# Memory's norm moved from the last gate block into the gated and differential products, and the head turns put behind the gated blocks

## What is computed

```python
z = h @ w_in[l]
u_s, q, k, v, g = jnp.split(z, [COL_SSM, COL_Q, COL_K, COL_V], axis=-1)
ys = s5_branch(u_s, ...)
ys = jax.nn.gelu(ys)
ys = ys * jax.nn.sigmoid(ys @ w_glu[l] + b_glu[l])            # gated product
branch_a = ys @ w_ssm_proj[l]
ya = diff_attention(q, k, v, ...)                             # 8 heads, each normed and scaled
branch_b = ya @ w_da_proj[l]                                  # differential product
gates = jax.nn.sigmoid((g + b_gate[l]).astype(F32))
g_a, g_b = jnp.split(gates, 2, axis=-1)
merged = (g_a * branch_a + g_b * branch_b)
x = x + rms_norm(merged @ w_mix_out[l], norm_mix_post[l])
...
mem_n = rms_norm(mem, norm_mem[l])                            # memory's norm: 256 rows of 1024
kv = mem_n @ w_xkv
```

## Time and profile before

| | us |
|---|---|
| median of 3 runs (2285.89 to 2286.31) | 2285.9 |
| the profiled execution's own time | 2281.14 |
| its span | 2279.5 |
| PE busy in the span (95%) | 2162.6 |
| DVE, ACT, POOL busy | 1123.0, 1005.2, 792.6 |
| chain that ended last: PE's share | 77% |

### The profile page before, as it was taken

How to read it: one execution, slowest core, us unless ns; L and a number is a source line. 1 busy time by engine, 2 the same in 40 slices (tenths; PEclk the granted TensorE clock), 3 DMA queues, 4 the chain that set the end, 5 groups by cost and what they waited for, 6 DMA issues and landing times.

```text
span 2279.5 us, 31042 instructions
## 1 busy us (share of the span) xinstructions
PE 2162.6 (95%) x11196; PEld 1775.5 (78%) x11196; DVE 1123.0 (49%) x2003; ACT 1005.2 (44%) x1950; POOL 792.6 (35%) x347
## 2 busy tenths in 40 slices
PE   5999999799989989999998999999999999999997
PEld 4788888678887878888886877878777777777776
DVE  5789999452542356452436523222286623222374
ACT  5767777652343442222223333434633433444631
POOL 2511111334464134444442423232343432232342
PEclk9999999899999999999998999999999999999998
DMA  4211111233233122232322222222223222222221
GB/s 145 84 61 65 64 60 60 74 120 102 93 126 96 38 83 74 94 100 93 102 92 88 93 65 75 68 72 71 87 84 125 83 84 64 67 69 71 76 94 63
DMA packets 51732, 189.32 MB, mean 83 GB/s; under 512 B 6564, under 2 KB 7204, under 8 KB 51108
## 3 DMA queue, kind: packets, MB, share of 16 engines
q1 hardware_dynamic: 48096, 175.13, 23.8%
q10 hardware_dynamic: 2452, 6.88, 0.8%
q0 software_dynamic: 1072, 5.77, 0.7%
HBM read 185.66 MB, written 2.10 MB: 82 GB/s over the span
## 4 chain that ended last, share of the span: by engine, by line
PE 77%; DVE 10%; ACT 5%; issue 3%; DVEq 3%; POOL 2%; DMA 0%; ACTq 0%; POOLq 0%
PE bank L350 21%; PE bank L352 20%; PE bank L351 20%; PE bank L933 2%; PE bank L976 2%; POOL weight_lo L382 1%; PE bank L959 1%; ACT weight_hi L376 1%; DVE wide_region L2225 1%; ACT wide_region L1059 1%; DVE wide_region L2228 1%; PE bank L425 1%; DVE h_lo L399 1%; PE bank L604 1%; PE bank L637 1%
## 5 line engine op out<-in xcount | busy, mean ns | idle before, releaser
L382 POOL TENSOR_TENSOR weight_lo<-weight_slots,weight_hi 128x1024 fp32r<-128x1024 f32 x277 | 674.6, 2436 | 1045.5 <-ACT weight_hi L376 1039.9
L376 ACT ACTIVATE weight_hi<-weight_slots 128x1024 fp32r<-128x1024 f32 x272 | 288.0, 1059 | 806.0 <-PE bank L352 720.3
L350 PE MATMUL bank<-h_hi,weight_hi 128*128 128x512 f32 x1144 | 464.5, 406 | 4.3 <-issue 3.0
L351 PE MATMUL bank<-h_lo,weight_hi 128*128 128x512 f32 x1144 | 449.6, 393 | 0.0
L352 PE MATMUL bank<-h_hi,weight_lo 128*128 128x512 f32 x1136 | 446.5, 393 | 0.0
L350 PEld LDWEIGHTS bank<-h_hi,weight_hi 128*128 128x128 f32 x1144 | 217.2, 190 | 52.4 <-issue 4.7
L352 PEld LDWEIGHTS bank<-h_hi,weight_lo 128*128 128x128 f32 x1136 | 215.4, 190 | 46.6
L351 PEld LDWEIGHTS bank<-h_lo,weight_hi 128*128 128x128 f32 x1144 | 217.6, 190 | 40.9
L382 POOL TENSOR_TENSOR head_weight_lo<-weight_slots,head_weight_hi 128x1024 fp32r<-128x1024 f32 x28 | 67.1, 2399 | 282.7 <-DVE v_region L1703 133.1
L350 PE MATMUL bank<-h_hi,head_weight_hi 128*128 128x512 f32 x336 | 139.8, 416 | 5.9 <-DVE h_lo L399 3.4
L352 PE MATMUL bank<-h_hi,head_weight_lo 128*128 128x512 f32 x336 | 132.9, 396 | 0.0
(11 more groups left out here) (489 smaller groups left out, 4468.4 us busy)
## 6 DMA issues: line engine op xcount, KB each, us to landing
weight_slots<-weights SPq DMA_DIRECT2D x328, 512.0 KB, 3.4
wide_region<-cmp_w ACTq DMA_DIRECT2D x2, 2048.0 KB, 9.3
v_region<-ssm_bc POOLq DMA_DIRECT2D x8, 256.0 KB, 4.5
residual<-x_in POOLq DMA_DIRECT2D x1, 2048.0 KB, 8.7
out<-normed SPq DMA_DIRECT2D x4, 512.0 KB, 2.7
residual<-x_in SPq DMA_DIRECT2D x2, 512.0 KB, 5.2
residual<-x_in ACTq DMA_DIRECT2D x2, 512.0 KB, 9.7
v_region<-mem_in POOLq DMA_DIRECT2D x1, 1024.0 KB, 5.2
```

The source lines that it names most:

```text
L350: pe.matmul(to, w_h[:, k, :], hi[:, k, 0:width], start=(k == 0), stop=False)
L351: pe.matmul(to, w_h[:, k, :], lo[:, k, 0:width], start=False, stop=False)
L376: act.activation(parts[0][s % 2], slot[s], ACT.Copy).then_inc(w_hi[s], 1)
L382: eng.tensor_tensor(parts[1][at], slot[s], parts[0][at].bitcast(F32), ALU.subtract).then_inc(w_lo[s], 1)
```

## The change

The same instructions are issued, in another order on four engines, and with waits placed accordingly. No size, buffer, DMA or shape changes.

- PE: `norm_sums` moves from between gate blocks 1 and 2 to behind the gated product, `norm_spread` from between gate blocks 2 and 3 to between the second and third block of Q_DA. The turns of heads 2s and 2s + 1 go from ahead of gated block s to behind it.
- ACT: the gate blocks' roundings and `gate_b` are spread out: two between the halves of `s5_back_in_time` and behind it, one in the middle of the gelus, one at their end. The squares of memory move behind gated block 3. `ya_hi` of two heads goes behind the sigmoid of its block. The roundings of `memn_hi` move into the differential product.
- DVE: the adding of the squares goes behind `glu(5)`, `norm_root` behind `glu(7)`; `glu(s)` goes ahead of the two `ya_lo`; the `YS2_LO` remainders are split four and four around the first differential block, and memory's split (`memory_split`) is spread over blocks 2 to 6 of it.
- POOL: `norm_power(pool, 1)` moves from the last gate blocks to between the weights of Q_DA.
- The stage numbers of the semaphores (`S_YS2`, `S_MEMN`) change places.

```diff
@@ -64,7 +64,7 @@
 
 FF_ORDER = ((1, 0), (1, 1), (2, 0), (1, 2), (2, 1), (1, 3), (2, 2), (2, 3))
 
-S_H0, S_YSG, S_YA, S_MEMN, S_YS2, S_MG, S_HX, S_OX, S_HF, S_L2 = (KT * i for i in range(10))
+S_H0, S_YSG, S_YA, S_YS2, S_MEMN, S_MG, S_HX, S_OX, S_HF, S_L2 = (KT * i for i in range(10))
 S_T, S_H, S_OBR, S_ACC, SL = (KT * i for i in range(5))
 QL = 19
 Q_END = Q_L2 + LAYERS * QL
@@ -685,12 +685,10 @@
             da_values(HEADS - 1, 3)
 
             gemm(pe, Q_GB + 1, 0, H1_HI, H1_LO)
-            gemm(pe, Q_GB + 1, 1, H1_HI, H1_LO)
-            norm_sums(pe, 1, 2, 2, MSQ)
-            gemm(pe, Q_GB + 1, 2, H1_HI, H1_LO)
-            norm_spread(pe, 1, 2)
-            gemm(pe, Q_GB + 1, 3, H1_HI, H1_LO)
+            for s in range(1, 4):
+                gemm(pe, Q_GB + 1, s, H1_HI, H1_LO)
             for s in range(4):
+                gemm(pe, Q_GLU, s, YSG_HI, YSG_LO, T, S_YSG if s == 0 else None)
                 for h in (2 * s, 2 * s + 1):
                     pe.wait_ge(head_scaled, h + 1)
                     if h >= 4:
@@ -698,10 +696,15 @@
                     for t in range(TT):
                         mm = pe.transpose(bank[2 + h % 4][:, t * P:(t + 1) * P], YA[:, h, t * P:(t + 1) * P], ident)
                     mm.then_inc(head_turned, 1)
-                gemm(pe, Q_GLU, s, YSG_HI, YSG_LO, T, S_YSG if s == 0 else None)
             for s in range(4):
                 gemm(pe, Q_GLU + 1, s, YSG_HI, YSG_LO)
-            both(pe, Q_DA, YA_HI, YA_LO, S_YA)
+            norm_sums(pe, 1, 2, 2, MSQ)
+            for s in range(4):
+                gemm(pe, Q_DA, s, YA_HI, YA_LO, T, S_YA if s == 0 else None)
+                if s == 1:
+                    norm_spread(pe, 1, 2)
+            for s in range(4):
+                gemm(pe, Q_DA + 1, s, YA_HI, YA_LO)
             both(pe, Q_SSM, YS2_HI, YS2_LO, S_YS2)
             both(pe, Q_MIX, MG_HI, MG_LO, S_MG)
             norm_sums(pe, 2, 3)
@@ -1205,7 +1208,12 @@
                 da_copy(b, 3)
                 if last:
                     head_out(b)
-                    s5_back_in_time(b, range(PPB))
+                    s5_back_in_time(b, range(2))
+                    ahead(act, Q_GB + 1, 0)
+                    gate_b(4)
+                    s5_back_in_time(b, range(2, PPB))
+                    ahead(act, Q_GB + 1, 1)
+                    gate_b(5)
 
             def last_weight_hi(s):
 
@@ -1222,32 +1230,29 @@
 
             act.drain()
             for k in range(KT):
-                if k % 4 == 0:
-                    ahead(act, Q_GB + 1, k // 4)
-                    gate_b(4 + k // 4)
+                if k == 4:
+                    ahead(act, Q_GB + 1, 2)
+                    gate_b(6)
                 act.activation(YSG_HI[:, k, :], U[:, k, :], ACT.Gelu_apprx_tanh).then_inc(hi_ready, 1)
                 act.activation(U[:, k, :], U[:, k, :], ACT.Gelu_apprx_tanh).then_inc(t_ready, 1)
-            act.wait_ge(mem_loaded, 16)
-            squares(act, MEMRAW, MEM, MSQ)
-            for blk in range(6, KT):
-                ahead(act, Q_GB + 1, blk % 4)
-                gate_b(blk)
+            ahead(act, Q_GB + 1, 3)
+            gate_b(7)
             act.drain()
             for blk in range(KT):
                 s = blk % 4
-                if blk < 4:
-                    for h in (2 * s, 2 * s + 1):
-                        act.wait_ge(head_turned, h + 1)
-                        act.activation(YA_HI[:, h, :], bank[2 + h % 4][:, :], ACT.Copy, scale=HN08).then_inc(hi_ready, 1)
                 if blk == 4:
-                    for k in range(KT):
-                        round_hi(act, S_MEMN, k, MEMN_HI[:, k, :], MEMN[:, k, :])
+                    act.wait_ge(mem_loaded, 16)
+                    squares(act, MEMRAW, MEM, MSQ)
                 ahead(act, Q_GLU + blk // 4, s)
                 act.wait_ge(mm_done[s], Q_GLU + blk // 4 + 1)
                 if blk >= 2:
                     act.wait_ge(ys_ready, blk - 1)
                 act.activation(PAIR[blk % 2], bank[s % 2][:, :], ACT.Sigmoid,
                                bias=column(V_BGLU + blk)).then_inc(evac_done[s], 1)
+                if blk < 4:
+                    for h in (2 * s, 2 * s + 1):
+                        act.wait_ge(head_turned, h + 1)
+                        act.activation(YA_HI[:, h, :], bank[2 + h % 4][:, :], ACT.Copy, scale=HN08).then_inc(hi_ready, 1)
                 if blk >= 4:
 
                     act.activation(R[:, 4 * s * T:4 * (s + 1) * T], R[:, 4 * s * T:4 * (s + 1) * T],
@@ -1256,6 +1261,8 @@
                 round_hi(act, S_YS2, k, YS2_HI[:, k, :], YS2[:, k, :])
             for blk in range(KT):
                 ahead(act, Q_DA + blk // 4, blk % 4)
+                for k in (2 * blk - 4, 2 * blk - 3) if 2 <= blk <= 5 else ():
+                    round_hi(act, S_MEMN, k, MEMN_HI[:, k, :], MEMN[:, k, :])
             for blk in range(KT + 1):
                 if blk < KT:
                     ahead(act, Q_SSM + blk // 4, blk % 4)
@@ -1864,9 +1871,6 @@
                 dve.wait_ge(evac_done[s], Q_GLU + blk // 4 + 1)
                 dve.tensor_tensor(U[:, blk, :], PAIR[blk % 2], U[:, blk, :], ALU.mult).then_inc(ys_ready, 1)
 
-            for k in range(1, KT - 1):
-                squares_added(dve, 1, k, MSQ, MEM)
-            norm_root(dve, 1, 2)
             dve.wait_ge(hpow_ready, 2)
             dve.tensor_tensor(HRT, HR0, HR0, ALU.mult)
             dve.drain()
@@ -1879,24 +1883,41 @@
                 by_row = HRS[:, TT * h:TT * h + TT].rearrange("p (t d) -> p t d", d=1).to_broadcast([P, TT, P])
                 dve.tensor_tensor(y, y, by_row, ALU.mult).then_inc(head_scaled, 1)
             for s in range(4):
+                glu(s)
                 for h in (2 * s, 2 * s + 1):
                     dve.wait_ge(hi_ready, S_YA + (h + 1))
                     dve.scalar_tensor_tensor(YA_LO[:, h, :], bank[2 + h % 4][:, :], HN08, YA_HI[:, h, :].bitcast(F32),
                                              ALU.mult, ALU.subtract).then_inc(lo_ready, 1)
-                glu(s)
             dve.sem_inc(t_ready, KT)
-            norm_split(dve, 1, S_MEMN, MEMN, MEMN_HI, MEMN_LO, MEMRAW, vec(V_MEM), MEM)
             for blk in range(4, KT):
                 glu(blk)
+                if blk == 5:
+                    for k in range(1, KT - 1):
+                        squares_added(dve, 1, k, MSQ, MEM)
             dve.drain()
             dve.sem_inc(t_ready, KT)
-            for k in range(KT):
-                rest_lo(dve, S_YS2, k, YS2_LO[:, k, :], YS2[:, k, :], YS2_HI[:, k, :])
+            norm_root(dve, 1, 2)
+
+            def memory_split(k):
+
+                if k < KT:
+                    dve.scalar_tensor_tensor(MEMN[:, k, :], MEMRAW[:, k, :], column(V_MEM + k), bank[7][:, 0:MEM],
+                                             ALU.mult, ALU.mult).then_inc(t_ready, 1)
+                if k >= 2:
+                    rest_lo(dve, S_MEMN, k - 2, MEMN_LO[:, k - 2, :], MEMN[:, k - 2, :], MEMN_HI[:, k - 2, :])
+
             dve.wait_ge(gates_done, 4)
             for blk in range(KT):
                 s = blk % 4
+                for k in range(4 * blk, 4 * blk + 4) if blk < 2 else ():
+                    rest_lo(dve, S_YS2, k, YS2_LO[:, k, :], YS2[:, k, :], YS2_HI[:, k, :])
                 dve.wait_ge(mm_done[s], Q_DA + blk // 4 + 1)
                 dve.tensor_tensor(MG[:, blk, :], RB[:, 8 + blk, :], bank[s % 2][:, :], ALU.mult).then_inc(evac_done[s], 1)
+                if blk == 2:
+                    dve.wait_ge(bc_ready, 2)
+                for k in (2 * blk - 4, 2 * blk - 3) if 2 <= blk <= 6 else ():
+                    memory_split(k)
+            dve.sem_inc(bc_used, 1)
             for blk in range(KT + 1):
                 if blk < KT:
                     s = blk % 4
@@ -2314,7 +2335,6 @@
 
             head_power(0)
             weight_lo(pool, Q_GB + 1, 2)
-            norm_power(pool, 1, 2)
             head_power(1)
             weight_lo(pool, Q_GB + 1, 3)
             weight_lo(pool, Q_GLU, 0)
@@ -2331,16 +2351,18 @@
                     for s in range(4):
                         weight_lo(pool, quad, s)
 
-            def root_within(quad, *norms):
+            def root_within(quad, *norms, tiles=TT):
 
                 for s in range(2):
                     weight_lo(pool, quad, s)
                 for n in norms:
-                    norm_power(pool, n)
+                    norm_power(pool, n, tiles)
                 for s in (2, 3):
                     weight_lo(pool, quad, s)
 
-            weights_lo(Q_GLU + 1, Q_KX)
+            weights_lo(Q_GLU + 1, Q_DA)
+            root_within(Q_DA, 1, tiles=2)
+            weights_lo(Q_DA + 1, Q_KX)
             root_within(Q_KX, 2)
             weights_lo(Q_KX + 1, Q_VX + 1)
             root_within(Q_VX + 1, 3)
```

## The result

Four executions of the changed kernel took 2263.18, 2256.35, 2265.85 and 2253.98 us, median 2259.76; four of the kernel before, beside them, 2285.89 to 2286.31. The profiled execution took 2263.18 us.

A forecast was written before the change was run, and what follows sets the result against it. PE, busy 95% of the span, was taken as the bound, its idle and low-clock time as the cost. Gains of 20.85 us less new waits of 0.2, 1.3 and 0.1 gave 19.3: 2285.9 to 2266.6 us, range 2264.2 to 2270.5.

The forecast's parts named there:

- Terms 1 to 3: Gate block 2 following block 1 at once, 14.68 us; norm_sums at full clock, 0.85; gate block 2 at full clock, 1.66.
- Terms 4 and 5: PE's waits for POOL's weight_lo before 490.12 and 513.42 in the differential product go: 2.27 and 1.4 us.
- ACT's walk: ACT's instruction list timed from 422.58; gated block 0 wanted at 433.20, with 0.2 us of new wait.
- First head turns: PE wants to turn head 0 at 438.83, starts at 439.9 after DVE's scaling: new wait 1.3 us.
- Third differential block: End of the re-ordered stretch: starts at 494.1 instead of 513.42, with 0.1 us of new wait.
- The hold: POOL's remainder, 436.5 to 438.9, makes DVE's two-input SBUF instructions wait to its end; first scaling done about 439.8.
- The covers: Thinnest: bank 1 behind YS2_LO freed at 498.9, wanted at 499.6. Rival that thin covers fail: 1.5 to 4 us, chance 0.13.
- POOL ahead of head 1: Rival: POOL's remainder for gated block 2 precedes head 1's scaling, which waits out 2.4 us: 2269.0, chance 0.12.
- Not what it says: Rival: ACT's list, not the norm, is the bound; PE's 14.5 us return behind the gelus: 2282 to 2286, chance 0.04.
- Slower by the clock: Rival: PE's new short waits drop its clock, 4.9 us more a block, five blocks: 2291, chance 0.03.
- behind 494 every row stands 19.3 earlier: Sign: after the third differential block all rows keep the 19.3 us; a shrinking gap means something later gives it back.

The follow-up runs named there:

- b_again: The kernel before, unchanged, run once more with a profile on chip A: 12 executions, mean 2276.9 us, ratio 0.9985.
- the two filled kernels: Changed kernel with filler matmuls in sixteen waits and a split moved later, 2237.3 us; kernel before with fillers in the same waits, 2259.2 us.

## Why the prediction was wrong, point by point

**The step that failed is the base.** "The runs' median lies 4.8 us above (2285.9), and I subtract the same 19.3." The three executions agreed within 0.4 us and were taken for the kernel's time. The term was to be the kernel's time and measured 2280.9, the mean of 68 executions that reach from 2270 to 2287: it was 5.0 us too high. The profiled execution, 4.8 us below the median, was the visible sign. With it right, 2280.9 - 19.3 = 2261.6, against 2259.8 of the first four executions and 2260.0 of all sixteen.

**The range failed with it.** It held costs of waits (2264.2 to 2270.5) and "a little for the unknown share between profile and median". A median of four executions with a standard deviation of 4 to 5 us moves by 2 or 3 us by itself. From the mean base, and with that, it would have been some 2256 to 2268 (an estimate made afterwards). The result compares two sets of four, and the 26 us between them are as much a matter of the draw: about 5 of them are the base, about 21 the change.

**The gain, 19.3.** Right to within 2 us: 20.9 (standard error 1.2) by all executions, 20.2 to 21.3 by the two filled kernels, 17.8 in the stretch of the first pair of profiles.
- Terms 1 to 3 (14.68, 0.85, 1.66): as forecast in the first pair. PE busy all of 423 to 437, clock 1.00 behind. Term 3 is the first profile's; in b_again the low clock behind this wait costs 0.84 more.
- Terms 4 and 5 (2.27, 1.4): term 4's wait is gone; term 5's is back at the same block with 1.50 or 0.31. Term 4 was undersized: behind this wait the clock fell too in three of four profiles, for 1.6 us. That is of the size of the mean's excess over 19.3 (1.6, standard error 1.2), which is no proof of it.
- ACT's walk: roundings forecast for 422.58, 429.7, 435.4 and 438.9, found at 422.42, 429.60, 435.28, 439.03; gated block 0 forecast for 433.20 plus 0.2, found at 433.19 without a wait. Right.
- First head turns: 439.9 forecast, 439.67 found; the turns are over at 440.69 (440.95 in the walk), so the new wait with its start is 440.69 - 438.54 - 0.23 - 0.90 = 1.0, not 1.3. `norm_sums` stands behind the gated product without a wait, the differential product starts at 482.38 (482.7 in the walk). The words of the walk, "gated block 1, then three times 6.34, the turns' 0.90, four blocks", add up to more than its 481.6, which is three times 6.34 and four blocks from 440.95.
- Third differential block: 494.1 forecast with 0.1 of wait; found 495.50 and 1.50, or the same with 0.31. The hold was drawn in one direction only, POOL over DVE. It works in the other too, and over four instructions.
- The covers: bank 1 behind `YS2_LO` did hold in every profile, no wait of DVE's multiply reached PE.

**Rivals.** POOL ahead of head 1: it came at 440.18, the second scaling had begun; right not to be expected. "Not what it says" fell by PE's busy 14 us. "Slower by the clock": its size is out, but its mechanism is real, only not caused by the change; "after the 2.0 us of idle before 490.12 the clock stayed at 1.00" was one execution's outcome, and the row at 701.63 of the same profile speaks against it. That behind 494 every row stands 19.3 earlier: 18.0 in the first pair.

## What to carry to other kernels

Three executions within 0.4 us don't make a base: lay the profiled execution beside them, and where it lies several us off, take the scatter of executions into the base and the range before any term of the change. On a kernel that PE bounds, sum the waits of 1 to 5 us and look for a granted clock under 1.00 behind each; matmuls that keep PE at work in them (into a bank that is overwritten anyway, and fewer than fill the wait) gained as much here (21 to 23 us) as the re-ordering (20 to 21) and made the time steadier. Where DVE has a run of two-input instructions from SBUF, put POOL's critical one ahead of the run or split the run, since either engine may have to wait for the other.

## What the runs showed of the hardware that I had not expected

- One program on one chip took from 2270.0 to 2286.9 us, and the mean granted clock (0.983 to 0.974) accounts for it, 1.8 us for each 0.001.
- The clock fell to its lower level (a matmul of 128x512 at 0.63 instead of 0.39 us on the row) behind a wait of 0.95 us, with more than 12 us of matmuls at 1.00 ahead of it, and stayed at 1.00 behind one of 2.00 us in one profile of four.
- POOL, due while DVE ran four `tensor_tensor` back to back, got in 0.56 us late in two profiles (2.96 us on the row) and stood until the run of four was over in three (4.1 us), with the same 0.58 us between the starts in the two shown above.
